# Residual and block outputs of the second half with tokens on partitions, and the norm's factor in a diagonal

## What is computed

```python
x = rmsnorm(x, final_norm_w)
for i in range(2):
    sh_m, sc_m, gt_m, sh_f, sc_f, gt_f = split(silu(c) @ ada_w[i] + ada_b[i], 6)
    h = rmsnorm(x, norm_g[i, 0]) * (1 + sc_m) + sh_m
    y = rglru_mixer(h) if i == 0 else gla_mixer(h)       # each ends in "@ w_out", 1024 x 1024
    x = x + gt_m * rmsnorm(y, norm_g[i, 1])
    h = rmsnorm(x, norm_g[i, 2]) * (1 + sc_f) + sh_f
    y = conv_ffn(h)                                       # up to 2 x 2816, conv, gelu(g) * v, down to 1024
    x = x + gt_f * rmsnorm(y, norm_g[i, 3])
return x
```

## Time and profile before

| | us |
|---|---|
| median of 3 runs | 1830.52 |
| lowest, highest | 1828.93, 1831.45 |
| span of the profiled execution | 1829.2 |
| TensorE busy | 1773.9 |
| VectorE busy | 1444.0 |
| ScalarE busy | 895.3 |

### The profile page before, as it was taken

How to read it: one execution, slowest core, us unless ns; L and a number is a source line. 1 busy time by engine, 2 the same in 40 slices (tenths; PEclk the granted TensorE clock), 3 DMA queues, 4 the chain that set the end, 5 groups by cost and what they waited for, 6 DMA issues and landing times.

```text
span 1829.2 us, 29668 instructions
## 1 busy us (share of the span) xinstructions
PE 1773.9 (97%) x11376; PEld 1568.9 (86%) x11376; DVE 1444.0 (79%) x2514; ACT 895.3 (49%) x1530; POOL 0.2 (0%) x4
## 2 busy tenths in 40 slices
PE   6999999999999999999999999999999989999998
PEld 3788887777888887988978999988999979989998
DVE  7799985558899998797866899878887478869864
ACT  4322325456323324443455745676656466567553
POOL 0000000000000000000000000000000000000000
PEclk8999999999999999999999999999999999999999
DMA  9582222112777776443321598552555625226543
GB/s 338 191 297 92 92 70 70 47 58 74 246 242 256 252 253 244 152 157 112 120 93 59 192 330 296 165 171 92 186 189 168 196 70 161 93 93 208 185 158 120
DMA packets 242045, 301.19 MB, mean 165 GB/s; under 512 B 5985, under 2 KB 223329, under 8 KB 241521
## 3 DMA queue, kind: packets, MB, share of 16 engines
q1 hardware_dynamic: 241904, 299.29, 49.7%
HBM read 298.22 MB, written 1.05 MB: 164 GB/s over the span
## 4 chain that ended last, share of the span: by engine, by line
PE 43%; DVE 8%; ACT 4%; issue 3%; DMA 0%; DVEq 0%; ACTq 0%
PE bank L626 10%; PE bank L628 10%; PE bank L631 10%; PE bank L602 2%; PE bank L603 2%; PE bank L604 2%; ACT w_hi L1247 2%; DVE w_lo L1957 1%; PE bank L962 1%; PE bank L963 1%; PE bank L964 1%; DVE stats L1858 1%; PE bank L1038 1%; PE bank L685 1%; DVE arena L2683 0%
## 5 line engine op out<-in xcount | busy, mean ns | idle before, releaser
L1957 DVE TENSOR_TENSOR w_lo<-ring,w_hi 128x1024 fp32r<-128x1024 f32 (+2 forms) x444 | 499.8, 1132 | 210.8 <-ACT w_hi L1247 207.7
L1247 ACT ACTIVATE w_hi<-ring 128x1024 fp32r<-128x1024 f32 (+2 forms) x444 | 434.3, 985 | 168.2 <-PE bank L631 98.9
L626 PE MATMUL bank<-h_hi,w_hi 128*128 128x256 f32 (+2 forms) x2366 | 418.3, 319 | 0.4
L631 PE MATMUL bank<-h_hi,w_lo 128*128 128x256 f32 (+2 forms) x2366 | 410.4, 315 | 0.0
L628 PE MATMUL bank<-h_lo,w_hi 128*128 128x256 f32 (+2 forms) x2366 | 410.3, 315 | 0.0
L626 PEld LDWEIGHTS bank<-h_hi,w_hi 128*128 128x128 f32 x2366 | 344.9, 188 | 35.5 <-issue 2.7
L628 PEld LDWEIGHTS bank<-h_lo,w_hi 128*128 128x128 f32 x2366 | 346.0, 188 | 29.8
L631 PEld LDWEIGHTS bank<-h_hi,w_lo 128*128 128x128 f32 x2366 | 346.0, 188 | 29.7
L1233 ACT ACTIVATE work<-bank 128x512 f32<-128x512 f32 (+1 forms) x138 | 68.5, 510 | 267.4 <-PE bank L631 203.4
L1233 ACT ACTIVATE arena<-bank 128x256 f32<-128x256 f32 (+4 forms) x125 | 56.6, 454 | 211.4 <-PE bank L631 147.8
L2264 DVE SCALAR_TENSOR_TENSOR arena<-arena,params 128x512 f32<-128x512 f32 (+1 forms) x240 | 130.3, 610 | 0.0
(11 more groups left out here) (301 smaller groups left out, 2244.5 us busy)
## 6 DMA issues: line engine op xcount, KB each, us to landing
ring<-in_w_in SPq DMA_DIRECT2D x86, 1024.0 KB, 5.8
arena<-in_ada_w_t SPq DMA_DIRECT2D x96, 512.0 KB, 5.9
ring<-in_ffn_w_up SPq DMA_DIRECT2D x44, 1024.0 KB, 5.1
ring<-in_w_branch SPq DMA_DIRECT2D x32, 512.0 KB, 4.7
arena<-in_w_mod_t SPq DMA_DIRECT2D x32, 512.0 KB, 5.2
ring<-in_ffn_w_down SPq DMA_DIRECT2D x16, 1024.0 KB, 5.2
ring<-in_gla_w_in SPq DMA_DIRECT2D x12, 1024.0 KB, 5.3
ring<-in_w_out SPq DMA_DIRECT2D x8, 1024.0 KB, 6.2
```

The lines of the kernel that those rows point to most:

```text
L626: pe.matmul(out[:, 0:n], w[0][:, k, :], hi(k, n), start=k == 0, stop=False)
L631: m = pe.matmul(out[:, 0:n], w[1][:, k, :], hi(k, n), start=False, stop=k == tiles - 1)
L1247: nc.scalar.activation(w_hi[u % PARTS][:, 0:src.shape[1], :], src, ACT.Copy)\
L1957: step(nc.vector.tensor_tensor(w_lo[u % PARTS][:, 0:nk, :], src, w_hi[u % PARTS][:, 0:nk, :].bitcast(F32), ALU.subtract), f"lo {u}", *(["u ...
```

## The change

From the end of the rg mixer on, x is kept with tokens on partitions, in the half of `xT` that held the context. `turn_x` brings it there after the last `rgg` product, ScalarE evacuates the banks (once as they are, once squared with a sum per token), and the final norm is a per-token factor times a row of weights that a new transfer brings (`fin_row`). All four blocks' output products take the form of the last FFN's. For the two mixers' products the first chunk goes channel tile by channel tile through both token tiles. At a seam (`boundary`) each token tile gets its sum, root and reciprocal as one column; x is added to in rows; the next norm's factor is written into a diagonal (`row_scale`), and sixteen fp32 matmuls of x against it (`norm_turned`) bring the normed x back with channels on partitions, where VectorE applies gain and shift and ScalarE and VectorE split it. Gain rows are now made for each of the four blocks. The `gla z` products go between the products of the first two GLA units. `pre_norm`, `store_y`, `sum_pairs`, `sum_y`, `post`, `normed2` and the early unit splits beside the fin norm are taken out. The diff, cut (helpers whose names say what they do are left out):

```diff
+            def gain_rows(tag):
+                pe.wait_ge(*scalar.did(f"row diag {tag}"))
+                for i in range(2):
+                    out = open_bank(f"gain row {tag}.{i}")
+                    for j in range(4):
+                        m = pe.matmul(out[:, P * j:P * j + P], ones_pp, row_diag[:, 512 * i + P * j:512 * i + P * j + P],
...
+            def norm_turned(name, idle):
+                outs = []
+                for t in range(ST):
+                    keep_clock(idle[t])
+                    pe.wait_ge(*vector.did(f"row scale {name}.{t}"))
+                    for k in range(KT):
+                        if t == 0 and k % 2 == 0:
+                            outs.append(open_bank(f"{name} turned {k // 2}"))
+                        m = pe.matmul(outs[k // 2][:, S * (k % 2) + P * t:S * (k % 2) + P * t + P], x_block(t, k),
+                                      row_scale(t), start=True, stop=True)
+                        if t and k % 2:
+                            m.then_inc(*tensor.does(f"filled {name} turned {k // 2}"))
+            def rows_out(tag, chunks, part, ready, by_tile):
...
+                    for k0, k1, names in chunks(c):
+                        units = [unit(name) for name in names]
+                        slot = unit_of[names[0]] % PARTS
+                        def products(k, t):
                             out = outs[t][:, 0:2 * P].rearrange("p (a n) -> p a n", a=2)
                             rows = slice(P * t, P * t + P)
-                            for k in range(k0, min(k0 + 8, FT)):
+                            hi, lo = (w[:, slot:slot + 2, k - k0, :] for w in w_parts)
+                            pe.matmul(out, part(h_hi, k)[:, rows], hi, start=k == 0, stop=False)
+                            pe.matmul(out, part(h_hi, k)[:, rows], lo, start=False, stop=False)
+                            return pe.matmul(out, part(h_lo, k)[:, rows], hi, start=False, stop=k == k1 - 1 and k1 == chunks(c)[-1][1])
...
+                        if c == 0 and by_tile:
...
+                                ready(k)
+                                for t in range(ST):
+                                    m = products(k, t)
...
+                        for t in range(ST):
+                            for k in range(k0, k1):
                                 if c == 0 and t == 0:
-                                    both_parts("ff 1")(k)
...
+                                    ready(k)
+                                m = products(k, t)
...
             def ffn(l):
-                keep_clock(9)
-                sum_pairs(f"n3 {l}")
-                if l:
-                    for i in range(4):
-                        turn_x(i)
-                keep_clock(3 if l else 7)
+                norm_turned(f"n3 {l}", (2, 2))
+                keep_clock(2)
...
+            def block_out(tag):
+                rows_out(tag, block_chunks(tag), lambda h, k: h[:, k, S:2 * S], both_parts(tag), True)
...
+            for i in range(4):
+                turn_x(i)
+            gain_rows("rg")
+            block_out("rg")
+            gain_rows("ffn 0")
             ffn(0)
...
-            keep_clock(9)
-            sum_pairs("n2 1")
-            keep_clock(7)
+            gain_rows("gla")
...
+            def z_product(k):
+                pe.wait_ge(*vector.did(f"full n2 1.{k}"))
+                m = pe.matmul(z_bank[0:16, 0:S], wz[:, k, :], pair_tile(k), start=k == 0, stop=k == KT - 1)
+                if k == KT - 1:
+                    m.then_inc(*tensor.does("filled gla z"))
+            project_group(["glaq 0", "glaq 1"], S, both_parts("n2 1"), before=z_product)
...
-                for n in range(GLA_H):
-                    project(f"gla{nm} {n}", S, ready=both_parts("n2 1") if nm == "q" and n == 0 else None)
+                for n in range(2 if nm == "q" else 0, GLA_H):
+                    project(f"gla{nm} {n}", S)
...
-            for i in range(2):
-                gain_rows(i)
             keep_clock(7)
-            block_out("gla", both_parts("gla"))
+            block_out("gla")
+            gain_rows("ffn 1")
             ffn(1)
...
+                if name == "w rga":
+                    sp.wait_ge(*tensor.did("filled out 1.0"))
+                    sp.dma_start(fin_row, io["fin_row"]).then_inc(fin_landed, 16)
...
+            def row_sum(tag, c, t):
+                if c:
+                    act.wait_ge(*scalar.did(f"row sum {tag}.{c - 1}.{t}"))
+                sum_squares(bank(f"rows {tag}.{c}.{t}")[:, 0:S], tensor.did(f"filled rows {tag}.{c}.{t}"),
+                            act_t[t][:, 0:S], row_sums(t)[:, c:c + 1], f"row sum {tag}.{c}.{t}")
...
+            def x_sum(tag, t, h):
+                if t:
+                    act.wait_ge(*scalar.did(f"x sum {tag}.{t - 1}.{h}"))
+                sum_squares(x_half(t, h), vector.did(f"x {tag}.{t}.{h}"), two(act_t[2 + h]), x_sums(t)[:, h:h + 1],
+                            f"x sum {tag}.{t}.{h}")
...
+            def boundary(tag, name, first, gain):
+                row_sum(tag, 3, 0)
+                row_root(tag, 0)
+                x_sum(tag, 0, 0)
+                row_sum(tag, 3, 1)
+                row_root(tag, 1)
+                x_sum(tag, 0, 1)
+                split_to(unit_of[first] + 2)
+                x_root(tag, 0)
+                x_sum(tag, 1, 0)
+                x_sum(tag, 1, 1)
+                x_root(tag, 1)
+                gain_out(gain)
+                for k in range(KT):
+                    act.wait_ge(*vector.did(f"full {name}.{k}"))
+                    nc.scalar.activation(h_hi[:, k, 0:S], pair_tile(k), ACT.Copy).then_inc(*scalar.does(f"hi {name}.{k}"))
...
+            def block_rows(tag, first):
+                for c in range(4):
+                    split_to(unit_of[f"y {tag}.{2 * c + 3}"] if c < 3 else unit_of[first] + 1)
+                    if c < 3:
+                        for t in range(ST):
+                            row_sum(tag, c, t)
...
+                if l == 0:
+                    for n in range(KT):
+                        gain_diag("gla", n)
...
+                if l == 0:
+                    split_to(unit_of["glaq 1"])
+                    boundary(tag, "n2 1", "glaq 0", "gla")
...
-                nc.scalar.activation(fin_square(n), xT[:, n, 0:S], ACT.Square).then_inc(*scalar.does(f"sq fin.{n}"))
+                if n == 0:
+                    act.wait_ge(*vector.did("gain2 1"))
+                gain_diag("rg", n)
...
-            block_out("rg", xc, "rg_y", 0)
-            ffn(0, lambda k: vector.did(f"x rg.{k}"))
-            pre_norm("n2 1", lambda k: vector.did(f"x ffn 0.{k}"), 1, 0, "glaq 0", False)
+            for n in range(KT):
+                high_tile("rg", xc, "rg_y", n)
+                i = n // 2
+                if n % 2:
+                    t, h = i // 2, i % 2
+                    evacuate(f"x turned {i}", two(act_t[i]), ACT.Square, [f"fin sum {i}"], accum_out=x_sums(t)[:, h:h + 1])
+                else:
+                    evacuate(f"x turned {i}", x_half(i // 2, i % 2), ACT.Copy, [f"x raw {i}"], last=False)
+            gain_out("rg")
+            warm_sqrt("rg")
+            for n in range(KT):
+                gain_diag("ffn 0", n)
+            for t in range(ST):
+                x_root("fin", t)
+            block_rows("rg", "ffg 0.0")
+            boundary("rg", "n3 0", "ffg 0.0", "ffn 0")
+            ffn(0)
...
-            block_out("gla", gla_o, "gla_y", 1)
-            ffn(1, lambda k: vector.did(f"x gla.{k}"))
+            split_to(unit_of["y gla.3"])
+            for n in range(KT):
+                high_tile("gla", gla_o, "gla_y", n)
+            warm_sqrt("gla")
+            block_rows("gla", "ffg 1.0")
+            boundary("gla", "n3 1", "ffg 1.0", "ffn 1")
+            ffn(1)
...
+            def x_scaled(tag, name, t):
+                x_inverse(tag, t)
+                step(nc.vector.tensor_scalar(row_scale(t), ident, x_inv(t), None, ALU.mult), f"row scale {name}.{t}")
+            def boundary(tag, name, l, q, first):
+                row_totalled(tag, 0)
+                row_stored(tag, 3, 0)
+                row_inverse(tag, 0)
+                x_added(tag, 0, 0)
+                x_added(tag, 0, 1)
+                row_totalled(tag, 1)
+                row_stored(tag, 3, 1)
+                x_totalled(tag, 0, f"x sum {tag}.0.1")
+                row_inverse(tag, 1)
+                x_added(tag, 1, 0)
+                x_added(tag, 1, 1)
+                x_scaled(tag, name, 0)
+                x_totalled(tag, 1, f"x sum {tag}.1.1")
+                x_scaled(tag, name, 1)
+                split_to(unit_of[first] + 2)
+                gain, shift = gain2[l][:, q, :], mod2[l][:, 12 * q:12 * q + KT]
+                def low(k):
+                    low_part(f"{name}.{k}", h_lo[:, k, 0:S], pair_tile(k), h_hi[:, k, 0:S])
+                for k in range(KT):
+                    filled(f"{name} turned {k // 2}")
```

(69 more changed lines are left out.)

319 lines of the change are left out of this document (96 added, 223 removed).

## The result

Nine executions of the changed kernel took 1834.01 us in the median (1832.67 to 1837.02), nine of the kernel before 1830.52; the ratio is 1.0020 with an interval of 1.0012 to 1.0029. The change made the kernel 3.5 us slower. The profiled execution has a span of 1832.2 us, 3.0 more than that of before; it took 1834.01 us, the median. The forecast was +4.5 on that execution and 1835.0 as a median.

The account below looks back on a forecast made before the run. TensorE, busy 97% of the span, was taken as the bound. -7.2 + 10.0 + 1.9 + 4.9 - 2.0 + 2.1 - 5.2 = +4.5 us: 1833.7 on the profiled execution, 1835.0 as a median, range 1828.5 to 1841.

Parts of the forecast that it names:

- Part 1: Three seams: a shorter chain per token tile makes seam one -7.2 us and seam three -5.2, each 9.9 long.
- Rival B: The seams shrink to TensorE's own work on top of A: -1.4, -2.2, -1.4, to 1826.4 us; 12%.
- Part 2: First mixer's output products: TensorE stands 8.6 us for a late-split weight unit, +10.0, plus +1.9 for the clock.
- +11.9: First mixer's output products: forecast difference for the whole stage, +10.0 and +1.9 for the clock.
- Part 3: First FFN's down products in rows: +1.1, gain diagonals ahead of the fourth unit +2.3, a clock stretch +1.5.
- half of 3.3: First FFN's down products: clock loss after 3.3 us idle, taken as +1.5 us (0 to 1.7).
- Part 4: Into GLA: seam 23.0 against 23.4 us, projections done earlier, two waits; net -2.0, plus +2.1 for the clock.
- The clock term of +2.1: GLA: two idle stretches of about 2 us each cost clock, +2.1 us (0 to 3.4).
- waits of +4.0: GLA unit 4: TensorE waits 1.9 us for the high part and 2.1 for the low part.
- A: FFN down products, second seam, GLA unit 4: the clock holds, -3.6 us, 1831.4, not slower; 20%.
- C: Seams: each diagonal 3 us later because ScalarE serves squares, roots and a split in one queue, +9, 1844; 10%.
- D: Table switch in the first mixer's output stall costs ScalarE 1.3 us more than its row shows, 1836.3; 3%.

Follow-up runs that it names:

- The two edits: On the changed kernel, unit y rg.3 split ahead of the fin work: 1830.48 us; then also table switch, roots, scalings and gain diagonals behind later chunks' splits: 1822.78 us.
- the unit first: Changed kernel with unit y rg.3 split by both engines right behind the first mixer's last output parts, ahead of the fin work: 1830.48 us, ratio to before 1.0003.
- the side work later: As the unit first, with table switch, roots and scalings behind the third chunk's splits, gain diagonals behind the fourth's: 1822.78 us, ratio to before 0.9962.
- all queues together: Changed kernel plus the side work later, first-block gain diagonals later, two GLA units earlier and the fourth down unit split earlier: 1818.41 us, ratio to before 0.9933.
- the banks first: As all queues together, first two GLA projections evacuated before the alphas and seventh unit split ahead of the first level difference: 1815.57 us, ratio to before 0.9915.
- the last run: As the banks first, with seam filler behind both token tiles removed and 4 (6 into GLA) instead of 2 ahead: 1810.30 us, ratio to before 0.9890.

## Why the prediction was right, and where it was not

**The sign and the size** came out as forecast: gain at the seams, loss in three queues.

**Part 1, the seams.** The chain was right step by step. The diagonals of seam one were ready 4.1 and 5.6 us after the last product (4.3 and 5.8 in the forecast), TensorE stood 1.37 us (1.45). The seams came out at 9.5, not 9.9: the turned products of the first diagonal began at 4.2, and the four steps from there on (products, filler, products, filler) took 5.3 us and not 5.6. Rival B, seams at TensorE's own work, did not come true: TensorE waited 1.37 us for the first diagonal, and even without the filler behind (8.65 us) it still does. Part of the forecast's -7.2 was luck of the execution: its 17.1 us for seam one before held about 1.1 us of lower clock, which it did not name.

**Part 2, the wait of 8.6 us** measured 8.4, and its parts are in the timelines above: ScalarE came to the unit at 1245.8 (1246.5 forecast), VectorE to its part at 1248.8 (1249.5), each 0.7 us early like the whole stage. The two edits show that it is a matter of place: the same instructions behind the next splits cost nothing. The stage was forecast at +11.9 with its clock and measured +12.0. The second mixer's products came after a wait of 3.66 us (3.6 forecast), and the time from GLA to their end did not change (99.1), as forecast.

**Part 3, the down products.** The wait was forecast as 0.96 + 2.3 = 3.3 us and measured 3.29; moving the eight diagonals gave back just 2.3. The term that was mis-sized is the clock: "half of 3.3" was +1.5, it cost 2.9 in the changed kernel. The lower clock lasted until 5.7 us after the products resumed, and not 3.3. In the six experiments that keep the wait the stage took 67.9 us three times (a cost of 1.7) and 68.9 to 69.1 three times; so the same wait does not fix the size. What differs in the traces is when the clock fell: in the changed kernel and the three slower ones 0.7 to 1.2 us before the products resumed, and it stayed low for 6.8 us; in the three others it fell between 0.2 us before and 1.5 us after that, and stayed low for 3.4 us.

**Part 4, GLA, is the step that failed**, in two ways that partly cancel. The clock term of +2.1 was added to waits of +4.0, but they are not a sum. The stretch takes 26.7 us with a half-clock stretch at the third projection and one wait of 1.9 (the change and the run with later gain diagonals) and 26.7 us without it and with both forecast waits, 1.62 and 1.90 (the runs with the unit first, the side work later and more filler):

```profile
1500.21 1.21 PE L650 MATMUL bank<-h_hi,w_hi 128*128 128x256 f32 x8
1507.73 1.22 PE L650 MATMUL bank<-h_hi,w_hi 128*128 128x256 f32 x8 [1.62 <-ACT w_hi L1275]
1511.79 1.21 PE L655 MATMUL bank<-h_hi,w_lo 128*128 128x256 f32 x8 [1.90 <-DVE w_lo L1980]
```

(the run with more filler). What ends this stretch is VectorE's chain from the alphas; a slow TensorE ahead of it only fills its own wait. Where the clock fell behind the waits, as in the run without filler behind the diagonals, it cost 1.5 us on top (28.2). In the changed kernel the lower clock lay ahead of the wait:

```profile
1499.59 1.66 PE L650 MATMUL bank<-h_hi,w_hi 128*128 128x256 f32 x8
1501.05 1.91 PE L652 MATMUL bank<-h_lo,w_hi 128*128 128x256 f32 x8
1511.17 1.21 PE L655 MATMUL bank<-h_hi,w_lo 128*128 128x256 f32 x8 [1.91 <-DVE w_lo L1980]
```

So it did not fall behind one of these waits, as the forecast had it; it fell after 13.5 us of z, projection and alpha products in which TensorE never stood (what lowered it there is open):

```profile
1486.10:1499.60 13.50, 13.50 (x74) 1.00 0.25 78
```

The other miss is the z products. A step of one z product and six others took 1.44 us (1486.15 to 1487.59) and not 1.23; the first and the last of the six each took 0.1 longer than the next start in a row does. Eight steps are 1.6 us more. The sum also had 0.5 us on the path for the evacuation of z (zT), and there it was too dear: ScalarE did it by 1497.25, beside the last projection products, which end at 1497.7. Together seam two gained 5.2 instead of 6.0.

**Rivals.** A, the clock holds in the FFN and GLA: no at the down products (2.9 us), yes at seam two, where it stayed at 1.00, and in GLA it fell, but ahead of the wait, where it cost nothing. C, later diagonals: no. D, a dearer table switch: no; the load at 1241.66 took 1.28 us and the next instruction started 1.30 after it. The Trainium skill (ScalarE: Activation LUTs, What ACT_TABLE_LOAD costs) has a drain of about 1380 ns on top. The trace does not agree: behind every load of this execution after which ScalarE waits for no other engine and no transfer, the next instruction starts 1.29 to 1.38 us after the load did. The Trainium skill (TensorE: Matmul & The Clock Gate, HAM oscillation — how this bites in real kernels) says that a wait between short blocks of products, 3 to 5 us in its example, makes the next block start cold. The trace agrees for the waits of 8.4 and 3.3 us here; in two experiments with the wait of 3.3 the products resumed at 2.4 GHz and fell to 1.2 only 1.5 us later. Behind the shorter wait of 1.9 us the products ran at 2.4 GHz here and in four of the five other runs that have it.

That the sum fell within 1.5 us of the measured one owes something to terms that cancel: the down products were 1.25 us too cheap, seam two 0.8 too good, GLA 1.95 too dear, the two other seams 1.1 too dear, and -0.6 us lie in stretches for which nothing was forecast.

## What to carry to other kernels

When engines split or convert weights in program order between other work, list for each block of products the instructions that stand between the last use and the next needed unit; small side work (diagonals, roots, a table load) costs its full length there and nothing two units later. After such a wait is removed look at the next unit and then at the banks: three of the edits here mostly moved the wait on, and the gain came when the whole stage had been cleared. A lower clock ahead of a wait that another engine ends cost nothing here (26.7 us with it and without); before adding the two, see whether the one fills the other.

## What was not expected of the hardware

The kernel's clock varies from execution to execution: over 25 executions of the kernel before the mean granted clock ran from 0.993 to 0.998 and the time from 1825.7 to 1833.5 us, faster ones mostly with the higher clock. The change has 0.990 in the median against 0.995. Filling 0.9 to 1.7 us of each seam's idle time with matmuls did not move that, nor did taking 2.3 us of waiting out of the down products: in that run the clock fell at seam two instead, and so it did in the profiled executions of all queues together and of the banks first. In the last run, with TensorE's idle time at seam two cut from 2.4 to 0.65 us, it did not; one execution of each is profiled, so that this is a hint and not shown. In GLA it fell in four runs with no idle time ahead of it. What decides where the stretches at 1.2 GHz fall is open.

The same wait of 3.3 us was followed by 1.7 or by 2.9 us of lost clock in kernels whose first block is the same. A figure for the cost of one wait, read from one execution, is uncertain by that much.
